# One mixer of a two-model block on one Trainium2 core: its gate chain, scores and sums placed among the projection panels

## The chip, the cores and the metric

One core of a Trainium2 chip runs the whole program. The metric is the device time of one execution in microseconds (us), the median of several. The engines are TensorE (PE, with its weight loads shown apart as PEld), VectorE (DVE), ScalarE (ACT), GpSimd (POOL) and SyncE (SP), which issues the weight transfers.

## The reference

The program is a chain: one attention and recurrence block with a mixture of experts, then four layers of feed-forward, mixer, feed-forward. The mixers of layers 0 and 3 are the ones changed here, so the changed code runs twice (`r` is 0 and 1). For one of them, with 256 tokens, 1024 channels, 4 heads, keys of 128 and values of 256 elements:

```python
def mlstm_mixer(x, w_in, b_if, conv_w, norm_g, w_out):
    proj = x @ w_in
    qk, v, o, if_pre = jnp.split(proj, [2 * H * dk, 2 * H * dk + H * dv, 2 * H * dk + 2 * H * dv], axis=-1)
    qk = jax.nn.silu(causal_depthwise_conv_2(qk, conv_w))
    if_pre = ML_GATE_CAP * jnp.tanh((if_pre + b_if) / ML_GATE_CAP)
    i_log, f_pre = jnp.split(if_pre, 2, axis=-1)
    f_log = jax.nn.log_sigmoid(f_pre)
    h = mlstm_chunkwise(q * dk ** -0.5, k, v, i_log, f_log)
    h = head_rms(h).reshape(B, T, H * dv) * norm_g
    return (h * jax.nn.sigmoid(o)) @ w_out

# inside mlstm_chunkwise, b = cumsum(f_log), m_t a running maximum, for one chunk:
    s = einsum('bhtd,bhsd->bhts', q, k) * exp(log_d - m_t)      # log_d[t, s] = b[t] - b[s] + i[s], masked
    den = sum(s)
    h = num / maximum(abs(den), exp(-m_t))                       # num = s @ v
```

The kernel takes all 256 tokens as one chunk, so it carries no state. `head_rms` divides each head's row by its root mean square.

## The kernel before

All data stays on chip between the parts. Every float32 weight arrives in panels of 1 MB (`raw`), is split by ACT into a rounded part (`w_hi`, L286) and by DVE into the rest (`w_lo`, L291), and is multiplied in three products (L321 to L323). A ring of RING = 3 slots holds the panels: the slot of panel p is loaded, split and used, and the split of panel p+3 (`act_ahead`, `dve_ahead`) waits until PE has done panel p. Each engine works through its own instructions in the order written, and waits on counted semaphores: `tensor_done` counts the results of PE, `lo_made` the panels split, `evacuated[i]` the reads of accumulator bank i. A result numbered n lies in `bank[n % 4]` and may be written when result n-4 has been read. Four more banks, `acc[0]` to `acc[3]`, hold the sums of the output projection and, at the joints between parts, the transposes of the norm.

A mixer has 16 panels: v0 to v3, q0 to q3 (these hold q and k, with 2 blocks of 128 columns each), o0 to o3, and four of the output weight. `pe_ml` (L1792) issues in this order: v0 and v1 in halves inside the norm (`pe_cross_halves`), v2, v3, q0 to q3, o0 to o3, and then a serial tail of small results named in `ML_ORDER`: `if` (gate logits of 8 columns, `pe_narrow`), `b` (cumulative sums, L1808 to L1810), `gT` (L1814), `Mt` (L1818), the exponents `D0` to `D3` of the decays (L1822, L1824), the scores `S0` to `S3` (L1829, L1830), the denominators `den` (L1835 to L1837), the numerators `num0` to `num3` (L1843 to L1845), four transposes `turn0` to `turn3` (L1851), and then the output panels out0 to out3 (`pe_out_panels`, rows of 512 into acc).

`act_ml` (L1859) reads each projection (L1866 for v, L1870 for q, the sigmoid L1872 for o) and splits the next panel right after; then it does the four silus (L1878), tanh, exp, ln (L1881 to L1885), the decays' exps (L1891 to L1893), |den| (L1897), the numerators scaled by 1/den (L1904, into `scratch`), the squares of those (L1910), and the rounded part of the gated output (`mix_hi`, L1917). `dve_ml` (L1924) makes w_lo after each split, the four-tap convolutions of q0 to q3 between (L1937, L1939), then `z`, `e1`, `nb`, `g`, `gT`, the running maximum and `nM` (L1951 to L1965), `Mt` (L1967), the four products score times decay (L1974), 1/den (L1979, L1980), the scaling by the norm (L1985, on `scratch`, all heads before `scaled` is signalled), gate times norm (L1991, `out0` to `out3`) and the rest of the gated output (`mix_lo`, L1999, `low0` to `low3`). `pool_ml` turns mean squares into reciprocal roots (L2011, L2013). The weights' transfers are issued by SP in panel order, each when the panel three before it has been split.

Of the kernel before, what the change touches and what calls it, by code (L numbers as in the profile page):

```python
# [26 lines left out]
EPS = 1e-6  # L27
# [126 lines left out]
def block_kernel(nc, d, out, consts, decays):  # L154

    ctx = ExitStack()
    with ctx:
# [1588 lines left out]
        def pe_out_panels(pe, c, panels, ready, src):  # L1746
# [7 lines left out]
            def last_ready(i):  # L1754
# [15 lines left out]
        ml_dve = Steps("ml_dve", ["cleared", "conv0", "conv1", "conv2", "conv3", "z", "e1", "g", "nM", "m", "rd",  # L1770
                                  "scaled"] + [f"out{j}" for j in range(4)] + [f"low{j}" for j in range(4)])
        ml_act = Steps("ml_act", ["silu0", "silu1", "silu2", "silu3", "tanh", "exp", "ln", "em", "ad", "squares"])
# [15 lines left out]

        def ml_moved(c):
            c.p += 4; c.e += 4 + len(ML_ORDER); c.n += len(ML_ORDER)  # L1790

        def pe_ml(pe, c, r):  # L1792
            pe_cross_halves(pe, c)
            pe_project(pe, c, 4, pe_columns_tok, first=2)
            c.p += 4; c.n += 4; c.e += 4
            pe_project(pe, c, 8, pe_columns_T)
            c.p += 8; c.n += 8; c.e += 8
            for key, j in ML_RES.items():
                n = c.n + j
                b = bank[n % BANKS]  # L1800
                if key == "if":
                    pe_narrow(pe, n, 44 + 8 * r, 8)
                    continue
                pe_result_free(pe, n)
                h = int(key[-1]) if key[-1].isdigit() else None
                if key == "b":
                    ml_act.wait(pe, "ln", r)
                    pe.matmul(b[:, 0:4], C("tri"), ml_nl[:, 0, :], start=True, stop=True)  # L1808
                    pe.matmul(b[:, 4:8], C("ones"), ml_nl[:, 0, :], start=True, stop=False)
                    last = pe.matmul(b[:, 4:8], C("tri"), ml_nl[:, 1, :], start=False, stop=True)  # L1810
                elif key == "gT":
                    ml_dve.wait(pe, "g", r)
                    for t in range(TT):
                        last = pe.matmul(b[0:4, t * P:t * P + P], ml_g[:, t, :], ident, start=True, stop=True)  # L1814
                elif key == "Mt":
                    ml_dve.wait(pe, "nM", r)
                    for t in range(TT):
                        last = pe.matmul(b[:, 4 * t:4 * t + 4], ml_nM[:, t * P:t * P + P], ident[:, 0:4],  # L1818
                                         start=True, stop=True)
                elif key[0] == "D":  # L1820
                    for at, cols in ((0, T), (T, P)):
                        pe.matmul(b[:, at:at + cols], ident[:, h:h + 1].to_broadcast([P, P]), ml_nM[:, T - cols:T],  # L1822
                                  start=True, stop=False)
                        last = pe.matmul(b[:, at:at + P], ident, C("neg_st"), start=False, stop=True)  # L1824
                elif key[0] == "S":
                    if h == 0:
                        ml_act.wait(pe, "silu3", r)
                    q, k = ml_qk[:, h, :], ml_qk[:, 4 + h, :]
                    pe.matmul(b[:, 0:T], k[:, 0:P], q, start=True, stop=True)  # L1829
                    last = pe.matmul(b[:, T:384], k[:, P:T], q[:, P:T], start=True, stop=True)  # L1830
                elif key == "den":
                    for h in range(4):
                        wait_evacuated(pe, c.n + ML_RES[f"S{h}"])
                        one = C("ones")[:, 0:1]
                        pe.matmul(b[:, h:h + 1], ml_S[:, h, 0:P], one, start=True, stop=True)  # L1835
                        pe.matmul(b[:, 4 + h:5 + h], ml_S[:, h, P:T], one, start=True, stop=False)
                        last = pe.matmul(b[:, 4 + h:5 + h], ml_S[:, h, T:384], one, start=False, stop=True)  # L1837
                elif key.startswith("num"):
                    if h == 0:
                        for back in range(9, 13):  # L1840
                            wait_evacuated(pe, c.n - back)
                    v = slice(h * ML_DV, h * ML_DV + ML_DV)
                    pe.matmul(b[:, 0:T], ml_S[:, h, 0:P], ml_v[:, 0, v], start=True, stop=True)  # L1843
                    pe.matmul(b[:, T:2 * T], ml_S[:, h, P:T], ml_v[:, 0, v], start=True, stop=False)
                    last = pe.matmul(b[:, T:2 * T], ml_S[:, h, T:384], ml_v[:, 1, v], start=False, stop=True)  # L1845
                else:
                    ml_dve.wait(pe, "scaled", r)
# [11 lines left out]
        def act_ml(act, c, r):  # L1859
            act_cross(act, c, norm_col(3 * r, 2))  # L1860
            for j in range(12):
# [5 lines left out]
                elif j < 8:  # L1867
                    if j == 4:
                        ml_dve.wait(act, "cleared", r)
# [1195 lines left out]
```

## Time and profile before

| | |
|---|---|
| median of 3 runs | 2969.29 us (2963.32, 2969.29, 2969.39) |
| the profiled execution, device time | 2963.17 us |
| its span | 2961.4 us |
| busy share of the span | PE 94%, PEld 88%, DVE 55%, ACT 45%, POOL 4% |
| chain of work that ended last | PE 87%, DVE 6%, ACT 4%, issue 1%, POOL 1% |
| mean granted TensorE clock | 0.967 of full |

The device time is the span and 1.8 us around it. The two mixers lie at about 788 to 941 us and 2608 to 2760 us of the span. A number in a row's "us" column is the time of a group that follows without a break; the same group in the second mixer has the same durations within 0.1 us. A granted clock of 1.00 is the upper of TensorE's two levels (2.4 GHz), 0.50 the lower (1.2 GHz); a number between is a mixture over the stretch.

### The profile page before, as it was taken

How to read it: one execution, taken by the hardware profiler on the slowest of the kernel's cores; microseconds unless marked ns; L12 is line 12 of the kernel's file. 1: busy time of each engine (PE TensorE's matmuls, PEld its weight loads, DVE VectorE, ACT ScalarE, POOL GpSimd, SP SyncE). 2: the span in 40 equal slices, each digit the busy share in tenths (PEclk: the TensorE clock that was granted, in tenths of full speed). 3: DMA queues.
4: the chain of work that ended last, by engine and by line, in shares of the span. 5: the costliest groups of instructions: out<-in, count | busy, mean ns of one | idle time of the engine just before them, and what ended most of it. 6: DMA issues, size and time to landing. Idle time of an engine off the chain costs nothing.

```text
span 2961.4 us, 51769 instructions
## 1 busy us (share of the span) xinstructions
PE 2770.3 (94%) x22402; PEld 2604.5 (88%) x22402; DVE 1634.4 (55%) x1725; ACT 1319.5 (45%) x1560; POOL 115.0 (4%) x185
## 2 busy tenths in 40 slices
PE   4789999899998999997998999999999999997999
PEld 4669999889997999997897999999979999997898
DVE  3445588854554445458765545446555454463544
ACT  3435477643444334447323434334334344344433
POOL 0000000000000000000211000000000000000000
PEclk9889999999988999998999999999999999998999
DMA  5207599845551555553301555555535555552453
GB/s 165 72 23 238 174 346 353 295 164 187 165 167 65 193 184 173 189 179 100 129 4 46 195 187 184 188 184 174 177 126 173 189 167 189 182 178 83 150 185 128
DMA packets 377590, 492.13 MB, mean 166 GB/s; under 512 B 18872, under 2 KB 337760, under 8 KB 377408
## 3 DMA queue, kind: packets, MB, share of 16 engines
q1 hardware_dynamic: 365280, 479.23, 48.6%
q0 software_dynamic: 2192, 7.73, 0.8%
q10 hardware_dynamic: 9936, 2.47, 0.4%
q8 instruction: 147, 2.41, 0.3%
q14 instruction: 35, 0.29, 0.0%
HBM read 488.35 MB, written 1.05 MB: 165 GB/s over the span
## 4 chain that ended last, share of the span: by engine, by line
PE 87%; DVE 6%; ACT 4%; issue 1%; POOL 1%; ACTq 1%; DMA 0%; DVEq 0%; POOLq 0%
PE bank L321 19%; PE bank L323 19%; PE bank L322 19%; PE acc L321 7%; PE acc L322 7%; PE acc L323 7%; PE bank L2462 1%; ACT w_hi L286 1%; PE acc L569 1%; DVE X L480 1%; DVE act_lo L501 1%; ACTq L827 1%; PE bank L2439 1%; PE bank L2450 1%; PE bank L569 1%
## 5 line engine op out<-in xcount | busy, mean ns | idle before, releaser
L291 DVE TENSOR_TENSOR w_lo<-raw,w_hi 128x2048 fp32r<-128x2048 f32 x360 | 824.2, 2292 | 790.3 <-ACT w_hi L286 790.1
L321 PE MATMUL bank<-act_hi,w_hi 128*128 128x256 f32 x3592 | 1019.4, 284 | 9.8 <-DVE act_lo L2714 7.7
L323 PE MATMUL bank<-act_hi,w_lo 128*128 128x256 f32 x3592 | 1018.6, 284 | 0.0
L322 PE MATMUL bank<-act_lo,w_hi 128*128 128x256 f32 x3592 | 1018.5, 284 | 0.0
L286 ACT ACTIVATE w_hi<-raw 128x2048 fp32r<-128x2048 f32 x360 | 688.1, 1912 | 511.4 <-PE acc L323 265.5
L321 PEld LDWEIGHTS bank<-act_hi,w_hi 128*128 128x128 f32 x3592 | 691.6, 193 | 13.3 <-issue 10.5
L322 PEld LDWEIGHTS bank<-act_lo,w_hi 128*128 128x128 f32 x3592 | 691.4, 192 | 2.9
L323 PEld LDWEIGHTS bank<-act_hi,w_lo 128*128 128x128 f32 x3592 | 691.4, 192 | 0.0
L321 PE MATMUL acc<-w_hi,mix_hi 128*128 128x512 f32 x928 | 366.0, 394 | 6.8 <-DVE mix_lo L1999 5.6
L322 PE MATMUL acc<-w_lo,mix_hi 128*128 128x512 f32 x928 | 364.8, 393 | 0.0
L323 PE MATMUL acc<-w_hi,mix_lo 128*128 128x512 f32 x928 | 363.8, 392 | 0.0
L321 PEld LDWEIGHTS acc<-w_hi,mix_hi 128*128 128x128 f32 x928 | 176.5, 190 | 42.5 <-issue 8.0
L323 PEld LDWEIGHTS acc<-w_hi,mix_lo 128*128 128x128 f32 x928 | 175.9, 190 | 37.8
L322 PEld LDWEIGHTS acc<-w_lo,mix_hi 128*128 128x128 f32 x928 | 176.5, 190 | 33.2
L704 ACT ACTIVATE silu_out<-bank 128x512 f32<-128x512 f32 x88 | 52.5, 597 | 299.7 <-PE bank L323 299.7
L321 PE MATMUL bank<-w_hi,act_hi 128*128 128x256 f32 x544 | 157.7, 290 | 1.2
L1506 DVE TENSOR_TENSOR w_lo<-raw,w_hi 128x2048 fp32r<-128x2048 f32 x57 | 130.6, 2292 | 49.8 <-ACT w_hi L1398 49.8
L322 PE MATMUL bank<-w_lo,act_hi 128*128 128x256 f32 x544 | 155.3, 285 | 0.0
L323 PE MATMUL bank<-w_hi,act_lo 128*128 128x256 f32 x544 | 155.0, 285 | 0.0
L1398 ACT ACTIVATE w_hi<-raw 128x2048 fp32r<-128x2048 f32 x57 | 109.0, 1913 | 38.7 <-PE bank L323 21.3
L749 DVE TENSOR_TENSOR gated<-silu_out,bank 128x512 f32<-128x512 f32 x88 | 60.5, 688 | 113.0 <-PE bank L323 113.0
L321 PE MATMUL bank<-w_hi,moe_xhi 128*128 128x256 f32 x384 | 109.6, 285 | 0.0
(492 smaller groups left out, 3252.3 us busy)
## 6 DMA issues: line engine op xcount, KB each, us to landing
raw<-in_ffn_w_gu SPq DMA_DIRECT2D x176, 1024.0 KB, 5.1
raw<-in_ffn_w_down SPq DMA_DIRECT2D x88, 1024.0 KB, 4.9
raw<-in_ml_w_in SPq DMA_DIRECT2D x24, 1024.0 KB, 5.4
raw<-in_rt_w_in SPq DMA_DIRECT2D x24, 1024.0 KB, 5.2
raw<-in_w_up SPq DMA_DIRECT2D x20, 1024.0 KB, 7.3
raw<-in_w_gate SPq DMA_DIRECT2D x19, 1024.0 KB, 6.8
raw<-in_w_down SPq DMA_DIRECT2D x18, 1024.0 KB, 6.6
moe_raw<-in_w_down SPq DMA_DIRECT2D x14, 1024.0 KB, 6.6
```

The source lines that it names most:

```text
L286: act.activation(w_hi[0:rows, slot, 0:size], raw[0:rows, slot, 0:size], ACT.Copy).then_inc(hi_made, 1)
L291: dve.tensor_tensor(w_lo[0:rows, slot, 0:size], raw[0:rows, slot, 0:size], w_hi[0:rows, slot, 0:size].bitcast(F32), ALU.subtract).then_inc ...
L321: pe.matmul(dst, l_hi, r_hi, start=start, stop=False)
L322: pe.matmul(dst, l_hi, r_lo, start=False, stop=False)
L323: return pe.matmul(dst, l_lo, r_hi, start=False, stop=stop)
L480: dve.scalar_tensor_tensor(x, scratch[:, t, cols], rstd[:, t:t + 1], x, ALU.mult, ALU.add).then_inc(x_quarter, 1)
L501: last = dve.scalar_tensor_tensor(act_lo[:, k, tok], turn_place(c, t, k), vecs[:, g + k:g + k + 1], act_hi[:, k, tok].bitcast(F32), ALU.mu ...
L569: last = pe.matmul(turn_place(c, t, k), X[:, t, k * P:k * P + P], diag[:, t, :], start=True, stop=True)
L704: act.activation(silu_out[:, h, :], bank[r % BANKS][:, :], ACT.Silu).then_inc(evacuated[r % BANKS], 1)
L749: dve.tensor_tensor(gated[:, h, :], silu_out[:, h, :], bank[b2][:, :], ALU.mult).then_inc(evacuated[b2], 1)
L1398: act.activation(w_hi[:, p % RING, :], moe_slab(p), ACT.Copy).then_inc(hi_made, 1)
L1506: dve.tensor_tensor(w_lo[:, p % RING, :], moe_slab(p), w_hi[:, p % RING, :].bitcast(F32), ALU.subtract).then_inc(lo_made, 1)
```

## The change

PE's order becomes: v0, v1, `if`, v2, v3, `b`, q0, `gT`, q1, `Mt`, D0, D1, q2, D2, D3, q3, o0, S0 to S3, o1, `den`, num0 to num3, o2, turn0 to turn3, o3, then the output panels as before. D, S and num of head h go to `acc[h]` and have no number in the ring of four banks; their readers signal by steps of `ml_act` and `ml_dve`. ACT and DVE are written out in the order that fits, each split of a panel standing where its projection's read stands (ACT) or where a line `ahead(...)` stands (DVE). The numerators stay in `acc[h]`: ACT takes the squares from there, scaled by 1/den (L1904 and L1910 become one pass), POOL multiplies the reciprocal root by 1/den, and one scaling by that product copies the numerators to `scratch`, heads 0 and 1 on ACT, heads 2 and 3 on DVE; each head's transposes wait for that head alone. `mix_hi` and `mix_lo` are made pair by pair. SP's order is unchanged.

```diff
@@ -1767,13 +1767,18 @@
...
+        ML_EV = [("v", 0), ("v", 1), ("if",), ("v", 2), ("v", 3), ("b",), ("q", 0), ("gT",), ("q", 1), ("Mt",), ("D", 0), ("D", 1),
+                 ("q", 2), ("D", 2), ("D", 3), ("q", 3), ("o", 0)] + [("S", h) for h in range(4)] + [("o", 1), ("den",)]
+        ML_EV += [("num", h) for h in range(4)] + [("o", 2)] + [("turn", j) for j in range(4)] + [("o", 3)]
...
+        ML_RES = {k: j for j, k in enumerate(k for k in ML_EV if k[0] not in ("D", "S", "num"))}
+        ML_PAN = {(x, j): 4 * i + j for i, x in enumerate("vqo") for j in range(4)}
+        ml_dve = Steps("ml_dve", ["cleared", "z", "e1", "g", "conv0", "nM", "conv1", "m", "conv2", "conv3"]
+                       + [f"S{h}" for h in range(4)] + ["rd", "scaled2", "scaled3"]
+                       + [x for j in range(4) for x in (f"out{j}", f"low{j}")])
+        ml_act = Steps("ml_act", ["tanh", "exp", "ln", "em"] + [f"D{h}" for h in range(4)] + [f"silu{j}" for j in range(4)]
+                       + ["ad"] + [f"squares{h}" for h in range(4)] + ["scaled0", "scaled1"] + [f"high{j}" for j in range(4)])
-        ML_ORDER = (["if", "b", "gT", "Mt"] + [f"D{h}" for h in range(4)] + [f"S{h}" for h in range(4)] + ["den"]
-                    + [f"num{h}" for h in range(4)] + [f"turn{j}" for j in range(4)])
-        ML_RES = {k: j for j, k in enumerate(ML_ORDER)}
...
         def ml_moved(c):
-            c.p += 4; c.e += 4 + len(ML_ORDER); c.n += len(ML_ORDER)
+            c.p += 12; c.n += len(ML_RES); c.e += len(ML_EV)
...
+            def project(x, j):
+                p = c.p + ML_PAN[x, j]
+                pe.wait_ge(lo_made, p + 1)
+                result(x, j)
+                done((pe_columns_tok if x == "v" else pe_columns_T)(pe, N[x, j] % BANKS, p % RING))
+
+            def decays(h):
+                b = acc[h]
...
+            pe_narrow(pe, N["if",], 44 + 8 * r, 8)
+            project("v", 2)
+            project("v", 3)
+            b = result("b")
+            ml_act.wait(pe, "ln", r)
...
+            done(pe.matmul(b[:, 4:8], C("tri"), ml_nl[:, 1, :], start=False, stop=True))
+            project("q", 0)
+            b = result("gT")
+            ml_dve.wait(pe, "g", r)
...
+            done(last)
+            project("q", 1)
+            b = result("Mt")
+            ml_dve.wait(pe, "nM", r)
...
+            done(last)
+            decays(0)
+            decays(1)
+            project("q", 2)
+            decays(2)
+            decays(3)
+            project("q", 3)
+            project("o", 0)
+            for h in range(4):
+                if h == 0:
+                    ml_act.wait(pe, "silu2", r)
+                elif h == 2:
+                    ml_act.wait(pe, "silu3", r)
+                ml_act.wait(pe, f"D{h}", r)
...
+            project("o", 1)
+            b = result("den")
+            ml_dve.wait(pe, "S3", r)
...
+            for h in range(4):
+                v = slice(h * ML_DV, h * ML_DV + ML_DV)
+                pe.matmul(acc[h][:, 0:T], ml_S[:, h, 0:P], ml_v[:, 0, v], start=True, stop=True)
+                pe.matmul(acc[h][:, T:2 * T], ml_S[:, h, P:T], ml_v[:, 0, v], start=True, stop=False)
+                done(pe.matmul(acc[h][:, T:2 * T], ml_S[:, h, T:384], ml_v[:, 1, v], start=False, stop=True))
+            project("o", 2)
+            for j in range(4):
...
+            project("o", 3)
...
+            def projected(x, j):
+                b = got(x, j)
...
+                read(last, x, j)
+                q = c.p + ML_PAN[x, j] + RING
+                act_split(act, q % RING, loads(q), E[x, j])
...
+            projected("v", 0)
+            projected("v", 1)
+            ml_dve.wait(act, "z", r)
...
+            projected("v", 2)
+            ml_dve.wait(act, "e1", r)
...
+            projected("v", 3)
+            projected("q", 0)
+            projected("q", 1)
+            ml_dve.wait(act, "m", r)
...
+            decays(0)
+            decays(1)
+            projected("q", 2)
+            decays(2)
+            decays(3)
+            projected("q", 3)
             for j in range(4):
                 ml_dve.wait(act, f"conv{j}", r)
...
+            projected("o", 0)
+            projected("o", 1)
+            b = got("den")
...
+                b = got("num", h)
+                    last = act.activation(ml_qk[:, 2 * h + t, :], b[:, t * T:t * T + T], ACT.Square,
+                                          scale=ml_rd[:, t, h:h + 1], accum_out=ml_ss[:, t, h:h + 1])
+                ml_act.done(last, f"squares{h}", r)
+            ml_pool.wait(act, "rs", r)
+            for h in range(2):
                 for t in range(TT):
-                    last = act.activation(ml_D[:, 0, 0:ML_DV], scratch[:, t, h * ML_DV:(h + 1) * ML_DV], ACT.Square,
-                                          accum_out=ml_ss[:, t, h:h + 1])
-                    if (h, t) != (3, 1):
-                        own_act(last)
-            ml_act.done(last, "squares", r)
-            for j in range(4):
+                    last = act.activation(scratch[:, t, h * ML_DV:(h + 1) * ML_DV], acc[h][:, t * T:t * T + T], ACT.Copy,
+                                          scale=ml_rs[:, t, h:h + 1])
+                ml_act.done(last, f"scaled{h}", r)
+            projected("o", 2)
...
+            high(0)
+            high(1)
+            high(2)
+            projected("o", 3)
+            high(3)
+            ml_moved(c)
             for j in range(2):
                 act_ahead(act, c.p + j, c.e + j)
...
+            ahead("v", 0)
+            b = got("if")
...
             ml_dve.done(dve.nop(), "z", r)
+            ahead("v", 1)
             ml_act.wait(dve, "exp", r)
...
+            ahead("v", 2)
+            ahead("v", 3)
+            b = got("b")
...
+            conv(0)
+            ahead("q", 0)
+            b = got("gT")
...
+            conv(1)
+            ahead("q", 1)
+            b = got("Mt")
...
             ml_dve.done(dve.nop(), "m", r)
+            conv(2)
+            ahead("q", 2)
+            conv(3)
+            ahead("q", 3)
...
+                b = got("S", h)
+                ml_act.wait(dve, f"D{h}", r)
...
+            ahead("o", 0)
+            ahead("o", 1)
             ml_act.wait(dve, "ad", r)
...
+            dve.nop().then_inc(evacuated[N["den",] % BANKS], 1)
             ml_pool.wait(dve, "rs", r)
+            for h in range(2, 4):
                 for t in range(TT):
+                    last = dve.tensor_scalar(scratch[:, t, h * ML_DV:(h + 1) * ML_DV], acc[h][:, t * T:t * T + T],
+                                             ml_rs[:, t, h:h + 1], None, ALU.mult)
+                ml_dve.done(last, f"scaled{h}", r)
+            ahead("o", 2)
...
+                wait_evacuated(dve, N["o", j])
+                b = got("turn", j)
...
+            for j in range(3):
+                out(j)
+                low(j)
+            out(3)
+            low(3)
+            ahead("o", 3)
...
-            ml_act.wait(pool, "squares", r)
-            own_pool(pool.tensor_scalar(ml_rs[:, :, :], ml_ss[:, :, :], 1.0 / ML_DV, EPS, ALU.mult, ALU.add))
-            flat = ml_rs[:, :, :].rearrange("p t h -> p (t h)")
-            ml_pool.done(pool.tensor_tensor(flat, flat, exponent[:, 0:8], ALU.pow), "rs", r)
-            c.p += 12; c.n += 12; c.e += 12
+            ml_act.wait(pool, "squares3", r)
+            ml_dve.wait(pool, "rd", r)
+            flat = lambda a: a[:, :, :].rearrange("p t h -> p (t h)")
+            own_pool(pool.tensor_scalar(flat(ml_ss), flat(ml_ss), 1.0 / ML_DV, EPS, ALU.mult, ALU.add))
+            own_pool(pool.tensor_tensor(flat(ml_ss), flat(ml_ss), exponent[:, 0:8], ALU.pow))
+            ml_pool.done(pool.tensor_tensor(flat(ml_rs), flat(ml_ss), flat(ml_rd), ALU.mult), "rs", r)
             ml_moved(c)
-            c.hi += 4
+            c.p += 4; c.e += 4
```

## Rows read from the trace of the kernel before

**Rows 1.** Windows from:to: length, PE, PEld, DVE, ACT, POOL busy, granted clock, DMA.

```profile
809.60:867.20 57.60, 57.60 (x483) 57.60 (x481) 37.64 (x43) 25.26 (x21) 0.00 (x0) 1.00 0.58 184
867.20:916.50 49.30, 31.20 (x176) 28.43 (x174) 13.59 (x33) 23.39 (x51) 1.86 (x2) 0.70 0.13 43
...
2686.80:2736.10 49.30, 31.20 (x176) 28.46 (x174) 13.59 (x33) 23.39 (x51) 1.86 (x2) 0.72 0.13 43
```

**Rows 2.** Timeline of PE: start, us, instruction, idle before and its releaser.

```profile
882.89 0.99 PE L1818 MATMUL bank<-con,ml_nM 128*128 128x4 f32 x4 [1.63 <-DVE ml_nM L1965]
...
888.89 0.60 PE L1822 MATMUL bank<-ml_nM,con 128*128 128x256 f32 x2
...
889.99 0.60 PE L1829 MATMUL bank<-ml_qk 128*128 128x256 f32 x2
...
892.61 0.28 PE L1835 MATMUL bank<-con,ml_S 128*128 128x1 f32 x2
...
895.21 0.68 PE L1843 MATMUL bank<-ml_v,ml_S 128*128 128x256 f32 x2
...
910.11 3.65 PE L1851 MATMUL bank<-con,scratch 128*128 128x128 f32 x16 [9.47 <-DVE scratch L1985]
916.55 0.77 PE L321 MATMUL acc<-w_hi,mix_hi 128*128 128x512 f32 x1 [2.79 <-DVE mix_lo L1999]
```

**Rows 3.** Windows of PE alone: length, PE busy, granted clock, DMA share, GB/s.

```profile
870.30:874.50 4.20, 4.20 (x21) 0.50 0.32 97
...
916.50:921.50 5.00, 4.95 (x12) 0.50 0.00 0
...
797.50:801.50 4.00, 3.97 (x23) 0.64 0.52 163
1143.60:1147.00 3.40, 3.40 (x28) 1.00 0.53 173
1470.30:1474.50 4.20, 4.19 (x74) 0.50 0.95 316
```

**Rows 4.** PE's waits over the span: us in total, times, longest.

```profile
PE acc L569 <- ACT gated L427: 48.5, 17, 11.3
...
PE bank L2439 <- DVE rw_xx L2820: 4.9, 1, 4.9
```

**Rows 5.** Timeline of ACT, first mixer.

```profile
867.40 0.60 ACT L1872 ACTIVATE ml_o<-bank 128x512 f32<-128x512 f32 x1 [3.36 <-PE bank L323]
867.89 1.90 ACT L286 ACTIVATE w_hi<-raw 128x2048 fp32r<-128x2048 f32 x1
869.81 1.28 ACT L1878 ACT_TABLE_LOAD   x1
871.11 2.19 ACT L1878 ACTIVATE ml_qk<-ml_qk 128x512 f32<-128x512 f32 x4
...
901.40 0.41 ACT L1910 ACTIVATE ml_D<-scratch 128x256 f32<-128x256 f32 x1
...
905.50 0.19 ACT L1910 ACTIVATION_READ_ACCUMULATOR ml_D<-scratch 128x1 f32 x1
```

**Rows 6.** Timeline of DVE, first mixer.

```profile
831.72 0.61 DVE L1937 TENSOR_SCALAR ml_qk<-ml_in,vecs 128x256 f32<-128x256 f32 x2
832.36 2.72 DVE L1939 SCALAR_TENSOR_TENSOR ml_qk<-ml_in,vecs,ml_qk 128x256 f32<-128x256 f32 x6
...
869.83 2.29 DVE L291 TENSOR_TENSOR w_lo<-raw,w_hi 128x2048 fp32r<-128x2048 f32 x1 [3.47 <-ACT w_hi L286]
...
881.31 0.41 DVE L1962 COPY ml_gT<-bank 4x256 f32<-4x256 f32 x1 [1.19 <-PE bank L1814]
...
907.77 2.19 DVE L1985 TENSOR_SCALAR scratch<-scratch,ml_rs 128x256 f32<-128x256 f32 x8 [11.62 <-POOL ml_rs L2013]
911.23 0.88 DVE L1991 SCALAR_TENSOR_TENSOR ml_o<-bank,vecs,ml_o 128x256 f32<-128x256 f32 x2 [1.27 <-PE bank L1851]
```

**Rows 7.** DVE scaling from a bank elsewhere: ns min/median/max, first and last start.

```profile
L2219 DVE TENSOR_SCALAR scratch<-bank,rt_rs x8: 743/746/752, 2161.6 to 2177.7; 128x512 f32<-128x512 f32 x8
```

More of the change, by code:

```diff
@@ L1796, in pe_ml @@
[L1796 to L1812, printed above, removed]
-                    for t in range(TT):
[L1814 to L1847, printed above, removed]
-                    for m in range(2):
-                        for t in range(TT):
-                            k = 2 * h + m
-                            last = pe.transpose(b[:, m * T + t * P:m * T + t * P + P],
-                                                scratch[:, t, k * P:k * P + P], ident)
-                last.then_inc(tensor_done, 1)
@@ new lines, in pe_ml @@
+            project("o", 2)
+            for j in range(4):
+                b = result("turn", j)
+                if j < 2:
+                    ml_act.wait(pe, f"scaled{j}", r)
+                else:
+                    ml_dve.wait(pe, f"scaled{j}", r)
+                for m in range(2):
+                    for t in range(TT):
+                        k = 2 * j + m
+                        last = pe.transpose(b[:, m * T + t * P:m * T + t * P + P], scratch[:, t, k * P:k * P + P], ident)
+                done(last)
@@ L1943, in dve_ml, with got, read @@
[L1943 to L1949 removed]
+            def got(*key):
+                dve.wait_ge(tensor_done, E[key])
+                return bank[N[key] % BANKS] if key in N else acc[key[1]]
+            def read(last, *key):
+                last.then_inc(evacuated[N[key] % BANKS], 1)
@@ new lines, in ahead, with conv @@
+            def ahead(x, j):
+                q = c.p + ML_PAN[x, j] + RING
+                dve_split(dve, q, q % RING)
+            def conv(j):
+                wait_evacuated(dve, N["q", j])
+                for tap in range(4):
+                    for k in (2 * j, 2 * j + 1):
+                        src, w = ml_in[:, k, tap:tap + T], V("ml_conv", (4 * r + tap) * 8 + k)
+                        if tap == 0:
+                            last = dve.tensor_scalar(ml_qk[:, k, :], src, w, None, ALU.mult)
+                        else:
+                            last = dve.scalar_tensor_tensor(ml_qk[:, k, :], src, w, ml_qk[:, k, :], ALU.mult, ALU.add)
+                    if tap < 3:
+                        own(last)
+                ml_dve.done(last, f"conv{j}", r)
@@ L1986, in dve_ml, with out @@
-            ml_dve.done(last, "scaled", r)
-            for j in range(4):
-                b, read = result(f"turn{j}")
+                    last = dve.tensor_scalar(scratch[:, t, h * ML_DV:(h + 1) * ML_DV], acc[h][:, t * T:t * T + T],
+                                             ml_rs[:, t, h:h + 1], None, ALU.mult)
+                ml_dve.done(last, f"scaled{h}", r)
+            ahead("o", 2)
+            def out(j):
+                wait_evacuated(dve, N["o", j])
+                b = got("turn", j)
```

166 lines of the change are left out of this document (72 added, 94 removed).

## The prediction, made before the changed kernel was run

> **What bounds the kernel now.** I read three views. The stretches first: from 809.6 us, where PE has finished v0 and v1, to 867.2 it works without a gap at the upper clock through ten panels (57.6 us, so 5.76 each), and ACT and DVE are busy 25.3 and 37.6 us of it. From 867.2 to the first output panel at 916.5 it is busy 31.2 of 49.3 us, at a mean clock of 0.70; the second mixer repeats this (31.2 of 49.3) [rows 1]. So a mixer has 18.1 us of idle PE, and the rest of its tail partly at the lower clock. The PE timeline says what the tail waits for: 9.47 us before the transposes, for the scaling by the norm; 2.79 before the output panels, for `mix_lo`; 1.63 before `Mt`; the rest of the 18.1 before `b` and `gT` [rows 2]. Each wait is a chain of short ACT, DVE and POOL work in which PE has nothing else to do. The clock comes third: the narrow product begins at 867.2 behind panels at the upper level, and from 870.3 to its end at 874.5 it runs at the lower, and the output panels run their first 5.0 us at the lower level [rows 3]. What matters is whether this work, put among the ten panels, finds cover, and what the panels then wait for.
>
> **What the full-clock work of the tail is.** At the upper clock one head of D takes 1.10 us (888.89 to 889.99), the four S 2.6, `den` 2.6, the four num 5.4 (895.21 to 910.11 less the wait of 9.47) [rows 2]. Groups like `Mt` take 0.99 at the lower clock [rows 2]; at the upper they are not shown, so each of `b`, `gT` and `Mt` lies between half and the whole, 0.5 to 1.0, and I take 0.5, for `b` 0.7. The transposes, 3.65 at the lower clock, come to between 1.8 and 3.65; I take 2.0 since the panels before them are at the upper level.
>
> **Walk, part 1: from 809.6 to the end of q0.** Before, v2 starts at 809.6; now `if` does. It took 7.3 us behind full-clock panels (867.2 to 874.5), ending at the lower level, and so will it here. v2 then starts low. Panels of this kind ran 5.0 us low after 916.5 before the clock rose, which costs half of that time [rows 3]; I charge 1.8, between 1 and 3. Sum: 7.3 + 1.8 + three panels (17.3) + `b` 0.7 = 27.1. Cover: tanh and exp run inside v2; ln stands behind v2's read and split on ACT (0.2 after PE, 0.49 to the split, 1.9, a table load of 1.28 [rows 5]), some 4.1 after v2's end, 1.6 before `b` asks for it. Behind ln's wait on ACT stands only v3's read. `g` stands on DVE behind the w_lo of v3's turn, 5.4 after v3's end against 6.5 at which `gT` asks: 1.1 to spare.
>
> **Part 2: from q0's end (call it 0) to o1's end.** A refill now: ACT reads at 0.2, splits at 0.7 to 2.6, DVE follows at 2.63 for 2.3 us [rows 5, 6], so a panel's successor is ready 4.9 after its end, and is wanted at 11.5 (two panels later) or more: 6.6 us to spare. PE does `gT` and q1 until 6.3. But DVE does conv0 first (it waits for the read of q0, 0.8; 3.4 long), then w_lo (2.2), and only then copies `gT` at 6.5. From that copy to `Mt` it is 1.58 (881.31 to 882.89) [rows 2, 6]. So `Mt` starts at 8.0: **a stall of 1.8 us**, once a mixer. Gaps of about 2 us stand before the norm's transposes in nearly all of the 17 joints [rows 4]; after some the clock fell (797.5: 0.64 over 4 us), after most it did not (1143.6: 1.00) [rows 3]. I charge 0.7. Then `Mt` 0.5, D0 and D1 2.2, q2, D2 and D3 2.2, q3, o0: 30.2. DVE, behind conv1 (3.4) and q1's w_lo, reads `Mt` at 13.6; ACT's em (with a table load) and the first exps end at 17.1, so q2 is read 0.45 late. conv3 ends at 28.7. Silus 0 to 2 follow q3's split and a table load and end near 30.0, the fourth at 30.6 [rows 5]: S0 is asked for at 30.2, so it just comes. S 2.6 and o1 5.76 end part 2 at 38.6; with the clock charge 39.3. The ring: the latest w_lo is q1's, ready 7.2 after q1's end instead of 4.9; the panel it serves is wanted 18 after. SP's transfers follow w_lo in the same order and are never later than the panels need.
>
> **Part 3: from o1's end (U) to o3's end.** PE: `den` 2.6, num 5.3 (the first one paid 0.1 for its start), o2: U+13.6. ACT reads o1, splits (to U+2.6), takes |den| at U+2.8; DVE's w_lo ends at U+4.9, 1/den is ready at U+5.3. Squares: eight took 4.29 us (901.40 to 905.69) [rows 5], here U+5.4 to 9.8, the last numerators being there at U+8. POOL took 2.1 from the squares to the next engine's start (905.69 to 907.77 [rows 5, 6]) and gets one small operation more, 0.2 to 0.5: rs at U+12.3. ACT scales heads 0 and 1 until U+13.9, DVE heads 2 and 3 until U+14.0. The 9.47 us wait is thus covered by o2, with nothing to spare. turn2 and turn3 end at U+15.5, turn3 having waited for ACT's read of o2 (behind its scalings). Then comes the **second stall**: o3 is numbered four behind turn0 and needs `out0` done, and DVE has the w_lo of o2's turn in front of it. ACT splits after its read of o2, U+14.4 to 16.3; w_lo to U+18.6; `out0` 0.9 and its signal [rows 6]; o3 starts at U+19.65, 4.2 us idle. After a wait of 4.95 the clock stood at 0.50 for 4.2 us [rows 3, 4], worth 2.1; I charge 2.0. o3 ends at U+25.4, or U+27.4 with it. In these 5.8 us `out0` to `out2` and their low parts are done, so out0's panel starts at once at the upper clock; `out3` and `low3` end 4 us later, out2's weights 6 us later, both wanted 10 later.
>
> **Sum.** New: 27.1 + 39.3 + 27.4 = 93.8 us from 809.6 to the first output panel. Before: 916.55 - 809.60 = 106.95. That is 13.15 less, and the output panels no longer start low, 2.5 in the first mixer; I take 2.1 as the mean of both, since the moment of recovery varies. 15.3 a mixer, 30.5 in all: **2963.2 - 30.5 = 2932.7** on the profiled execution's own time. Two of the three unprofiled runs lie 6 us above it (2969.3), one at it. The median after may fall in either place, 2932.7 or 2938.8; I name **2935**. Changes within 0.2% (6 us) are what a measurement of this kernel can't tell from none.
>
> **Rivals.**
> - *Stalls and clock cost half.* The clock recovers early behind `if`, o3 waits 2 us (DVE's w_lo in the shadow), no dip at `Mt`: 5 more a mixer, 2922 to 2928. For it: the charges of 1.8, 0.7 and 2.0 are estimates. Against: the order of DVE fixes the wait of o3. 12%. The end of this road is 81.5 us for the stage (panels 57.6, the rest 23.9 at full clock and no idle), 2908.
> - *The tight handovers slip.* ln to `b`, `g` to `gT`, silu2 to S0 and squares to turn0 have 1.6, 1.1, 0.2 and 0 us. If each is late by 1 to 2 and the clock falls once more, 7 to 8 a mixer go: 2948 on own time, to 2954. For it: two have no slack, and semaphore steps of 0.05 to 0.1 are not in my walk. Against: a slip at S0 or turn0 moves both queues alike. 20%. Here belongs the source of the scaling: from SBUF it took 2.19 for eight passes, 0.27 each, from a bank 0.747 for twice the columns [rows 6, 7], so some 0.4 a pass, which I used. The Trainium skill, VectorE: DVE Perf Modes, section "Why PSUM operands drop a tier", speaks against the move: a float32 tensor_scalar has its double rate from SBUF only. By it the four passes on DVE cost 0.5 more than from SBUF, and head 3 would be the last before turn3; the trace agrees on the rate.
> - *The panels wait for their splits; nothing is gained.* Each of seven w_lo stands behind an awaited result; were the waits 6.6 us longer than in my walk, each panel would stall. That takes 15 us a mixer and gives 2963 to 2969. My largest delay is 2.3. 5%.
> - *Slower: the clock stays low among the panels.* The short products and the stalls, spread over the stage, keep PE at the lower level. Panels at the lower level take twice as long, so it decides where 27% of the 57.6 us of panel work runs low (15.3); at half it is 28.8 - 15.3 = 13.5 slower a mixer, 2990. Against: PE ran D, S, `den` and num back to back at the upper clock, and after a 4.95 us wait it was low for 4.2 us only [rows 3, 4]. 3%.
>
> **How the numbers follow.** The forecast has 60%. Its own bounds, clock charges 1 to 3, 0 to 1.7 and 1 to 2.5, give 2927 to 2938 on own time, to 2944 with the 6 us. 10% of the slip and half of the first rival must be in too: 2921 to 2951. Faster 0.92, same 0.05, slower 0.03.
>
> **What would show it.** Right: PE's waits in the stage sum to about 6 to 7 us, before `Mt` (1.8, behind `nM`) and before o3 (4.2, behind `out0`'s bank); none before the transposes above 0.5; the narrow product again falls to the lower clock after 3 us; the first output panel starts some 93 us after v1's end. Wrong: waits before S0 or turn0 above 1 us; lo_made as PE's releaser among the panels; a mean clock under 0.85 over the stage.

## The result, and the profile after

The changed kernel takes 2935.01 us (median of 4 runs, 2929.75 to 2936.62); the kernel before, in the runs beside it, 2968.51. The ratio is 0.9888, 95% interval 0.987 to 0.9905: faster by 1.1%. The profiled execution took 2936.62 us. Two lines of the page, busy time and the chain that ended last:

```profile
PE 2768.2 (94%) x22402; PEld 2605.3 (89%) x22402; DVE 1632.4 (56%) x1717; ACT 1314.4 (45%) x1552; POOL 115.2 (4%) x187
...
PE 87%; DVE 6%; ACT 4%; issue 1%; POOL 1%; ACTq 1%; DMA 0%; POOLq 0%; DVEq 0%
```

PE issues the same 22402 products as before, and ACT and DVE have 8 instructions fewer each; what went is PE's idle time and its time at the lower clock. Where: PE's transposes of the norm (L569) stand at every joint between two parts, so the distance from one joint to the next times a part. The first mixer of the changed kernel lies between these two starts (timeline of PE; start, duration):

```profile
797.21 1.16 PE L569 MATMUL acc<-gated,X 128*128 128x128 f32 x8 [1.97 <-ACT gated L427]
...
925.55 1.16 PE L569 MATMUL acc<-gated,X 128*128 128x128 f32 x8
```

That is 128.34 us, against 143.49 before (797.53 to 941.02): 15.15 less. The second mixer went from 141.44 to 126.89: 14.55 less. Together 29.7, where the two spans differ by 26.6; the other stretches, unchanged in their code, gave back 3.1, in four steps of 1.3 to 2.2 against two of 1.4 the other way (below).

Inside the first mixer, stretches of the changed kernel (length; PE, PEld, DVE, ACT, POOL busy; granted clock; DMA share; GB/s), which answer to [rows 1]: the gate logits with v2; then all to the end of o1; then `den` to the end of o3:

```profile
809.30:825.10 15.80, 15.80 (x99) 15.80 (x98) 4.58 (x4) 4.10 (x5) 0.00 (x0) 0.68 0.46 136
825.10:875.70 50.60, 49.33 (x400) 48.34 (x399) 32.45 (x49) 27.01 (x32) 0.00 (x0) 1.00 0.42 128
875.70:903.50 27.80, 23.80 (x163) 22.97 (x162) 10.96 (x17) 12.24 (x28) 2.07 (x3) 0.88 0.31 110
```

From the end of v1 to the first output panel it is 94.2 us, where it was 106.95. And PE's waits of that stage, first mixer (us in total, times, longest), where [rows 2] had 18.1 us of idle time:

```profile
PE bank L321 <- DVEq L2069: 4.0, 1, 4.0
PE bank L1842 <- DVE ml_nM L2030: 1.3, 1, 1.3
```

Two waits are left, the two of the walk. The timeline of PE places them (start, duration, idle before):

```profile
816.94 0.56 PE L321 MATMUL bank<-w_hi,act_hi 128*128 128x256 f32 x1
...
845.17 0.58 PE L1842 MATMUL bank<-con,ml_nM 128*128 128x4 f32 x4 [1.27 <-DVE ml_nM L2030]
...
889.35 1.91 PE L1884 MATMUL bank<-con,scratch 128*128 128x128 f32 x16
895.26 0.55 PE L321 MATMUL bank<-act_hi,w_hi 128*128 128x256 f32 x1 [4.00 <-DVEq L2069]
903.50 0.40 PE L321 MATMUL acc<-w_hi,mix_hi 128*128 128x512 f32 x1
```

The transposes follow o2 with no wait at all, where 9.47 us stood. o3 starts at 895.26 after 4.00 idle. What DVE does meanwhile (its timeline):

```profile
887.18 1.66 DVE L2056 TENSOR_SCALAR scratch<-acc,ml_rs 128x256 f32<-128x256 f32 x4 [6.21 <-POOL ml_rs L2097]
891.98 2.29 DVE L291 TENSOR_TENSOR w_lo<-raw,w_hi 128x2048 fp32r<-128x2048 f32 x1 [3.14 <-ACT w_hi L286]
894.19 0.87 DVE L2066 SCALAR_TENSOR_TENSOR ml_o<-bank,vecs,ml_o 128x256 f32<-128x256 f32 x2
```

The bank that o3 needs is freed by the last of these lines; its input, turn0, had been there since about 889.9, and DVE stood 3.14 us in wait for a split that `out0` doesn't need.

The clock, in windows of PE alone (length, busy, granted clock, DMA share, GB/s): low from 2.7 us into the narrow product to 5.3 us into v2, low again over the end of the wait and most of o3, and at its upper level where the output panels begin, which ran low before [rows 3]:

```profile
812.00:822.20 10.20, 10.20 (x49) 0.50 0.46 127
...
893.90:900.70 6.80, 5.44 (x25) 0.50 0.48 157
...
903.50:908.50 5.00, 5.00 (x24) 1.00 0.00 2
```

### The profile page after: what moved, and what is told of

It is laid out like the page before. It is cut to its first block, busy times and chain, and to the rows that moved or that the text cites. A ratio compares the mean times of both kernels' runs of the same rounds, so it can differ in the third digit from the quotient of the medians.

```text
span 2934.8 us, 51755 instructions
## 1 busy us (share of the span) xinstructions
PE 2768.2 (94%) x22402; PEld 2605.3 (89%) x22402; DVE 1632.4 (56%) x1717; ACT 1314.4 (45%) x1552; POOL 115.2 (4%) x187
## 4 chain that ended last, share of the span: by engine, by line
PE 87%; DVE 6%; ACT 4%; issue 1%; POOL 1%; ACTq 1%; DMA 0%; POOLq 0%; DVEq 0%
PE bank L321 20%; PE bank L323 19%; PE bank L322 19%; PE acc L321 7%; PE acc L322 7%; PE acc L323 7%; PE bank L2545 1%; ACT w_hi L286 1%; PE acc L569 1%; DVE X L480 1%; DVE act_lo L501 1%; ACTq L827 1%; DVE w_lo L291 1%; PE bank L2522 1%; PE bank L2533 1%
## 5 line engine op out<-in xcount | busy, mean ns | idle before, releaser
L321 PEld LDWEIGHTS bank<-w_hi,act_hi 128*128 128x128 f32 x544 | 108.7, 200 | 3.7 <-issue 3.0
```

What stands on the lines that cost most here:

```text
L321: pe.matmul(dst, l_hi, r_hi, start=start, stop=False)
```

## The experiments

Times from joint to joint, first and second mixer, in us. In the first, several kernels also have a fall of the clock right at the leading joint, worth 1.4; the second has none there, so it is the cleaner column. The time of one whole execution is no measure of an edit: it moves by several us with falls of the clock elsewhere.

| kernel | first | second | second against changed |
|---|---|---|---|
| before | 143.49 | 141.44 | +14.55 |
| changed | 128.34 | 126.89 | 0 |
| changed, again | 128.20 | 127.74 | +0.85 |
| `out0` ahead of w_lo | 121.83 | 120.50 | -6.39 |
| scan ahead of convolution | 128.45 | 127.86 | +0.97 |
| gate logits woven into v2 | 122.18 | 121.12 | -5.77 |
| all three | 115.88 | 115.89 | -11.00 |
| gate chain only | 130.19 | 131.84 | +4.95 |
| norm only | 136.13 | 134.74 | +7.85 |
| two scalings | 126.15 | 124.83 | -2.06 |
| all three, again | 117.28 | 115.91 | -10.98 |
| two edits | 115.76 | 115.72 | -11.17 |
| two edits, `den` woven | 117.04 | 115.69 | -11.20 |
| all three, `den` woven | 114.22 | 114.18 | -12.71 |

**`out0` ahead of the w_lo.** Is the wait at o3 DVE's order, or the end of a chain?

```diff
-            ahead("o", 2)
...
             for j in range(3):
                 out(j)
+                if j == 0:
+                    ahead("o", 2)
                 low(j)
```

> DVE makes out0 (0.9 us) before the w_lo that stands in front of it. Theory A (DVE's own order holds the bank that o3 needs, and the idle time costs clock besides): PE's wait before o3 falls from 4.00 us to 0 to 0.5, o3 runs at the upper clock and takes 5.8 instead of 8.2 us, the output panels start 6.0 to 6.4 us earlier in each mixer, 12 to 13 us in all. Theory B (the wait is set by the chain of squares, root and scaling, and would only move): the wait stays above 2 us, before the transposes or before o3, and less than 5 us are gained in all.

One execution: 2916.27 us. Windows of PE over o2 and the transposes, then o3, then the first output panel:

```profile
883.40:891.20 7.80, 7.80 (x67) 1.00 0.20 82
891.20:897.00 5.80, 5.80 (x50) 1.00 0.27 89
897.00:902.00 5.00, 5.00 (x24) 1.00 0.32 112
```

No idle time and no low clock: o3 takes 5.8 us instead of 8.2, and the mixers are 6.5 and 6.4 shorter, 12.9 in all, which is theory A (the first lies 0.1 above its 6.4). Of the 6.4, 4.0 are the wait and 2.4 what it did to the clock. The whole execution is 20.4 shorter than that of the changed kernel; the other 7.4 lie in four stretches that the edit doesn't touch, each with less time at the lower clock, and are not its gain.

**The scan ahead of the convolution.** The order of `nM` and `conv0` changes places in the list of steps, and

```diff
-            conv(0)
-            ahead("q", 0)
             b = got("gT")
...
+            conv(0)
+            ahead("q", 0)
             conv(1)
```

> DVE copies gT and makes nM before the convolution of q0 and the w_lo that stood ahead of them. Theory A (queue order): the wait of 1.27 us before Mt is gone and nothing later moves, 1.3 us less in each mixer from the end of v1 to the first output panel, 2.5 in all. Theory B (the work put off comes due later): Mt starts earlier, but PE waits as long for w_lo, the silus or S3 further on, 0 gained.

One execution: 2935.82 us. The wait before `Mt` is gone: the page has one wait left in the stage, the 4.0 at o3. But the mixers got 0.1 and 1.0 longer. Windows of PE: o1, `den`, the first numerators, the rest of them:

```profile
868.40:874.30 5.90, 5.90 (x53) 1.00 0.51 188
874.30:876.90 2.60, 2.60 (x27) 1.00 0.87 356
876.90:880.30 3.40, 3.40 (x9) 0.50 0.11 7
880.30:884.00 3.70, 3.70 (x19) 1.00 0.72 277
```

Up to the end of the scores everything runs 1.47 us earlier (868.43 against 869.90). Then, behind the 2.6 us of one-column `den` products, the clock is at the lower level for 3.4 us, which costs 1.7. In the second mixer it falls 2.1 us after `den` has begun, for 6.8 us, which costs 3.3; there the fall at o3 is half as long and gives 0.9 back. Neither theory stands as written: no later wait took the gain, the clock did, in both mixers. In the changed kernel's two profiled executions the same products passed without a fall in three mixers and had one in the fourth (1.7 lost there and 0.9 given back at o3, the +0.85 of the table). I come back to it with the last two kernels.

**The gate logits woven into v2.** In `pe_ml`, per token tile and k, three narrow products and then v2's three:

```diff
-            pe_narrow(pe, N["if",], 44 + 8 * r, 8)
-            project("v", 2)
...
+            for t in range(TT):
+                for k in range(KT):
...
+                    last = split_product(pe, bi[:, t * 8:t * 8 + 8], act_hi[:, k, tok], act_lo[:, k, tok],
+                                         narrow_hi[:, k, a:a + 8], narrow_lo[:, k, a:a + 8], k == 0, k == KT - 1)
...
+                    last = split_product(pe, bv[:, t * PW:t * PW + PW], act_hi[:, k, tok], act_lo[:, k, tok],
+                                         w_hi[:, slot, w], w_lo[:, slot, w], k == 0, k == KT - 1)
```

> The 48 narrow products of the gate logits are issued in threes between the threes of v2 instead of in one block ahead of it. Theory A (the block of narrow products lets the clock fall, and v2 pays for it): both together take 11.2 us at the upper clock instead of 7.6 + 8.2, the chain to ln then ends 0.4 to 0.9 us after v3, so 3.7 to 4.3 us less in each mixer, 7.4 to 8.6 in all. Theory B (narrow products keep the clock low wherever they stand, or the block costs no clock): the granted clock over v2 stays below 0.9 and at most 2 us are gained in all.

One execution: 2922.93 us. Both together, and v3 behind them, in windows of PE:

```profile
808.10:819.20 11.10, 11.10 (x98) 1.00 0.41 128
819.20:825.00 5.80, 5.80 (x51) 1.00 0.39 117
```

11.1 us at the upper clock instead of 15.8 at 0.68: theory A. `b` follows v3 at once, so ln, which I had 0.4 to 0.9 late, was in time. The mixers gained 6.2 and 5.8, more than the 3.7 to 4.3 expected: 4.7 is this edit, the rest is clock elsewhere that this execution happened not to lose (at the joint ahead of the first mixer, and in half of the fall at o3 in the second).

**All three.**

> All three edits together. Theory A (they act in different places): the gains add up, 10.5 to 12 us in each mixer, so 21 to 24 us less than the changed kernel and 52 to 57 less than the kernel before, near 2912. Theory B (one critical chain behind all): the largest alone, 12 to 13 us.

2910.22 us, ratio to before 0.9827 (0.9805 to 0.985), which is 51.2 less than the kernel before on that chip, a little under the 52 expected. The mixers lose 12.5 and 11.0 us; 1.4 of the 12.5 is the fall at the leading joint, which this execution had not. So the first two edits add up (6.4 and 4.7), and they act in different places. What the scan adds to them the comparison with two edits says, below: nothing so far.

**Gate chain only.** Which part of the change brought what? PE's order `if` v2 v3 `b` q0 `gT` q1 `Mt` q2 q3 o0 to o3, then D, S, `den`, num, turn; the norm as in the changed kernel. The core of it:

```diff
+            project("q", 2)
+            project("q", 3)
+            project("o", 0)
+            project("o", 1)
+            project("o", 2)
+            project("o", 3)
             decays(0)
             decays(1)
-            project("q", 2)
             decays(2)
             decays(3)
-            project("q", 3)
-            project("o", 0)
```

> Only the gate chain stands among the panels; D, S, den, num and the transposes follow o3 as before the change, with the one scaling of the changed kernel. Theory A (walk of the queues: D 4.4, S 2.6 with a short wait for D's exps, den and num 7.8, some 4.4 of wait for squares, root and scaling, transposes, low0 ready 23 to 25 us after o3; the gate chain costs 12.9 among the panels): a mixer from joint to joint is 3 us longer than in the changed kernel and 12 shorter than before. So the placing of D, S and num behind the stall at o3 brings only 3 of the 15 us. Theory B (the tail's waits were what counted and they come back): 7 us or more longer than in the changed kernel.

One execution: 2950.31 us. 1.9 and 5.0 us longer than the changed kernel. The two differ by luck with the clock: the first mixer was spared the fall at the joint (1.4) and 3.4 us of low clock in the gate stage (1.7), and without that it is 5.0 as well. That is 2 more than theory A's 3, and short of theory B's 7. The wait before the transposes is 4.4 as walked. What the walk has not is a wait of 0.7 before `den`, and the clock, which in the second mixer is low for 6.8 us from 1.7 us into `den` and for 3.4 at the transposes. So placing D, S and num among the panels is worth 5 of the 14.6 us, not 3.

**Norm only.** PE's order of before, the new norm.

```diff
-            pe_narrow(pe, N["if",], 44 + 8 * r, 8)
             project("v", 2)
             project("v", 3)
...
+            project("o", 3)
+            pe_narrow(pe, N["if",], 44 + 8 * r, 8)
```

> PE's order is that of the kernel before; only the norm is changed (squares out of the accumulators, one scaling on two engines, transposes head by head, mix_hi and mix_lo pair by pair). Theory A: the wait before the transposes falls from 9.5 to 4.4 us, that before the output panels from 2.8 to under 0.5, 7 to 8 us less in each mixer than before, about half of the whole gain. Theory B (the norm's chain only gives the time to another wait): less than 3 us in each mixer.

One execution: 2947.27 us; 7.4 and 6.7 less than before in the mixers. Waits of PE in the first mixer:

```profile
PE bank L1883 <- ACT scratch L1959: 4.4, 1, 4.4
PE bank L1835 <- ACT ml_nl L1940: 3.7, 1, 3.7
...
PE acc L321 <- DVE mix_lo L2074: 0.2, 1, 0.2
```

4.4 instead of 9.5 and 0.2 instead of 2.8, as walked; a new wait of 0.7 stands before `den`. So the norm's part alone, without any new placing, is nearly half of the gain. Its own pieces (squares out of the accumulators, one scaling on two engines, transposes head by head, output pair by pair) were not run one by one in this order. In the second mixer, whose column has no spared falls, the shares are 6.7 for the norm, 2.9 more for the gate chain among the panels, 5.0 more for D, S and num (differences of the table's rows; the first mixer has 7.4, 5.9 and 1.9).

**Two scalings.** The changed kernel with 1/den applied on ACT, squares from SBUF, and DVE scaling all heads.

```diff
-                    last = act.activation(ml_qk[:, 2 * h + t, :], b[:, t * T:t * T + T], ACT.Square,
-                                          scale=ml_rd[:, t, h:h + 1], accum_out=ml_ss[:, t, h:h + 1])
+                    last = act.activation(scratch[:, t, h * ML_DV:(h + 1) * ML_DV], b[:, t * T:t * T + T], ACT.Copy,
+                                          scale=ml_rd[:, t, h:h + 1])
...
-            for h in range(2, 4):
+            for h in range(4):
```

> The changed kernel with two scalings again: numerators by 1/den into SBUF on ACT, squares from there, DVE scales all four heads. Theory A (in the new order DVE's w_lo sets the start of o3, so the longer chain is mostly covered): PE waits some 2.2 us before the transposes and 2.5 before o3 instead of 0 and 4.0, a mixer is 0.7 to 2 us longer. Theory B (the one scaling carries the gain here too): 5 us or more longer in each mixer.

One execution: 2935.34 us. Both theories miss: the mixers are 2.2 and 2.1 us shorter than with one scaling. Waits of PE, and the clock from o2's end over o3:

```profile
PE bank L321 <- DVEq L2065: 2.4, 1, 2.4
PE bank L1881 <- DVE scratch L2053: 1.4, 1, 1.4
```

```profile
883.00:900.00 17.00, 13.21 (x106) 1.00 0.29 102
890.00:902.00 12.00, 9.04 (x69) 1.00 0.27 89
```

The idle time is nearly the same, 3.8 against 4.0, but in two pieces, and the clock never falls; o3 takes 5.8 us. In the changed order the work saved on ACT and DVE was worth nothing, since DVE's w_lo stands at the end either way (it starts at 891.88 here and at 891.98 in the changed kernel), and joining two waits to one cost some 2.4. With the w_lo in front of `out0` the one scaling loses 2.1 us a mixer; with `out0` first the two scalings were not run.

**The changed kernel, two edits, and `den` woven.** Three kernels, timed in turn on one chip; the two edits are `out0` first and the woven gate logits.

> The changed kernel as it is, to be timed beside the next two: 0.9888 of the kernel before, between 0.987 and 0.9905.

2934.95 us, 0.9891 (0.9873 to 0.9908).

> out0 ahead of the w_lo, and the gate logits woven into v2; the convolution and the maximum in the order of the changed kernel. Theory A (the two act apart, as the single looks say: 6.4 and 6.0 us a mixer): 12 to 12.5 us less in each mixer, 24 to 25 less than the changed kernel, ratio to before 0.981 to 0.983. Theory B (moving the scan first helps too, and was hidden by the clock): 2 us or more slower than with all three edits.

2909.81 us, 0.9813 (0.9795 to 0.9831): faster than before by 1.9% and than the changed kernel by 25.1 us, as theory A has it (12.6 and 11.2 in the mixers, where it has 12 to 12.5; 1.4 of the 12.6 is again the joint). From just ahead of the gate logits to the end of the first output panel, in one window of PE:

```profile
806.00:897.00 91.00, 89.73 (x701) 1.00 0.44 139
```

One wait of 1.27 us and no fall of the clock. Against all three edits (2910.22, ratio 0.9827) there is no loss, so theory B's 2 us are not there. Its reason, a gain of the scan hidden by the clock, is another matter: the last kernel below shows it.

> As the one before, and the 24 products of one column of den stand in threes among the second half of o1, with |den| and 1/den ahead of the splits that follow o1. Theory A (the den block of 2.6 us lets the clock fall in some executions, 1.7 us each time, as behind den in the second look; woven it cannot): no fall of the clock between o1 and o2, equal work otherwise, 0 to 3.4 us less than without this edit, 1 to 2 in the median. Theory B (the clock falls by chance of phase whatever stands there): no difference, and the falls are found as often.

The edit puts three `den` products behind each second group of three of o1's second half:

```diff
+                    if m == 1 and k % 2:
+                        h = k // 2
...
+                        pe.matmul(bd[:, h:h + 1], ml_S[:, h, 0:P], one, start=True, stop=True)
```

2910.22 us, 0.98 (0.9781 to 0.9818): no difference from the two edits alone, and the 1 to 2 us that theory A expected are not seen. The profiled executions can't decide: neither of the two had a fall between o1 and o2. In the two kernels with the scan first, the clock fell during `den` or right behind it in all four mixers; in six profiled executions of kernels without it and with `den` in one block behind o1, in one of twelve. In the two kernels that keep `den` in the tail behind a wait of 0.7 us (gate chain only, norm only), it fell in all four, 1.7 to 4.0 us after `den` had begun.

**`den` woven where the clock fell.** All three edits again, and the same with `den` woven, timed in turn on one chip.

> All three edits a second time. In the two kernels that have the scan first, the clock fell behind den in all four mixers seen; in the others in one of twelve. Theory A (it belongs to this order of work): it falls again in both mixers, 115.9 us from joint to joint. Theory B (chance of the moment): it falls in none or one, and a mixer without the fall takes 114.3 to 114.6 us.

2913.16 us, 0.9814 (0.9795 to 0.9833). In its profiled execution the clock fell in both mixers again, and 115.91 us is the second mixer, as theory A has it (117.28 the first, with a fall at its leading joint). Windows of PE, first mixer: the end of `den` and the first numerator (`den` ends at 874.9), the next ones, the last ones with the start of o2:

```profile
873.50:875.90 2.40, 2.40 (x20) 1.00 0.50 205
875.90:879.30 3.40, 3.40 (x10) 0.50 0.25 46
879.30:883.00 3.70, 3.70 (x23) 1.00 0.59 241
```

> All three edits, and den woven into the second half of o1. Theory A (the block of one-column products lets the clock fall in this order, and woven it cannot): no fall from v2 to the first output panel, PE has no wait there, a mixer takes 114.3 to 114.6 us from joint to joint, 1.2 to 1.5 less than with any kernel so far; 2.5 to 3 us less than all three edits. Theory B (the fall needs no den block): the clock falls between o1 and o2 here too and nothing is gained.

2907.7 us, 0.981 (0.9788 to 0.9831). One window of PE from just ahead of the gate logits to the end of the first output panel:

```profile
806.00:897.00 91.00, 91.00 (x706) 1.00 0.44 139
```

PE is busy in every one of the 91 us and never leaves the upper clock; the mixers take 114.22 and 114.18, so theory A stands: the scan's 1.3 us is real, and the block of `den` products took it back through the clock. Why it does so in this order, six times in six, and once in twelve in the other, the runs don't say. The medians are 5.5 us apart (2913.16 and 2907.7), but the single times overlap (2906.38 to 2914.64 and 2905.13 to 2917.58), and they can't be told from those of two edits either (0.981 against 0.9813); only the profiled mixers show the 1.5 us.

## Why the prediction was right, step by step

The range held the time, and the walk held the mechanism. By its own steps, first mixer:

- *Part 1, 27.1 forecast, 28.1 measured* (809.30 to 837.37). The narrow product took 7.64 for 7.3, v2 8.15, so the clock's charge was 2.4 where I had 1.8: the stretch of low clock lasted into v2 for 5.3 us. In it v2's products of 256 columns came every 0.213 us, behind it every 0.120, so the low level took 1.8 times as long for them, not the twice that I used throughout. `b` took 0.6 for 0.7. The term was within its bounds of 1 to 3. The covers held: ln ended at 829.2, `b` was asked for at 830.85, so 1.6 to spare as said.
- *Part 2, 39.3 forecast, 38.4 measured.* The wait before `Mt` was 1.27 for 1.8, and my charge of 0.7 for the clock behind it was not incurred in either mixer. S0 came when asked for: it needs the first three silus, the four took from 865.51 to 867.70, so the third ended at about 867.15, and S0 began at 867.36 with no wait.
- *Part 3, 27.4 forecast, 27.8 measured.* No wait before the transposes; 4.00 for 4.2 before o3, behind `out0`'s bank; 2.4 for 2.0 lost to the clock in o3.
- *The output panels start at the upper clock.* Forecast 2.1 a mixer; L569 comes 22.05 us after their start where it was 24.47: 2.4. In the second mixer it is 22.06 for 23.76, 1.7, since these panels do differ between the mixers before; the mean is the 2.1.
- Sum of the two mixers: 30.5 forecast, 29.7 measured. The parts were off by up to 1 us, mostly in the clock charges (0.6 too low in part 1, 0.7 too high in part 2, 0.4 too low at o3), and these cancelled: the three charges were 4.8 us for 4.5. That they did is luck.
- *The signs.* The waits sum to 5.3 us, a little under the 6 to 7 named; both stand where they were said, and there is none before the transposes. The narrow product fell to the lower clock after 2.7 us, and the first output panel came 94.2 us after v1's end for "some 93".
- *A reading that was wrong.* I put gaps of about 2 us at nearly all of the 17 waits of the norm's transposes. Ten of them are of that length (1.95 to 1.98); the clock fell at four of the ten before and at five of the ten after. Nothing in the sum changes by it.
- *The rest of the kernel.* I had it unchanged. It gave back 3.1 us in the profiled execution: the clock fell at three joints at which it hadn't before (1.4 each) and stayed up at two at which it had fallen; the largest step, 2.2, lies inside another part (1318.8 to 1602.7). The window behind one joint, before and after:

```profile
1819.90:1823.40 3.50, 3.42 (x28) 1.00 0.64 167
```

```profile
1805.30:1808.70 3.40, 3.40 (x17) 0.50 0.66 198
```

  The feed-forward part behind the norm is then 188.1 us long instead of 186.7. In other runs such falls stand at other joints, so I take this for scatter of an execution, not for a cost of the change. It is of the size of the spread between runs (6.9 us among the four).
- That the median is 2935.01 and I wrote 2935 is partly luck: I split 6 us between two clusters of the times before, and the measured medians fell by 33.5 us while the two profiled executions differ by 26.6. With 29.7 for the mixers, both are inside that scatter.
- *Rivals.* Handovers slipping: none did, by any measurable amount. Weights as releaser among the panels: no such wait in the stage. A low clock among the panels: the gate stage and o3 only, mean 0.91 from 806 to 903.5 (the falls were mine, and in the sum). The rival of smaller stalls did not happen by itself, but the experiments made it: one stall and the narrow block went for 25.1 us in the medians (two edits), and with the other stall and the `den` block gone too, the stage from v1's end to the first output panel took 81.42 us (808.10 to 889.52). The rival's end of the road was 81.5 us and 2908; the median was 2907.7, on another chip than the changed kernel's.
- The source of the scaling. On "VectorE: DVE Perf Modes" in the Trainium skill, section "Why PSUM operands drop a tier": the trace agrees. Four passes from the accumulators took 1.66 us (L2056), 0.41 apiece, against 0.27 from SBUF [rows 6], 0.56 more for the four where I had 0.5; and it cost nothing, since they end at 888.84 and the transposes could not begin before 889.35.

What I had wrong in kind showed in the experiments, not in the forecast: I priced the clock by the length of a wait. The two scalings show that nearly the same idle time costs 3.8 us in two pieces and 6.4 in one.

## What to carry to other kernels

When serial small work is put among wide products, walk every in-order queue that it passes: here the remaining waits both came from DVE work placed ahead of the one short step that PE needed, and moving one line ahead of another was worth 6.4 us a mixer. Look at what a block of very narrow products does to TensorE's clock and to the wide products behind it; woven in threes among wide ones the gate logits cost their own time only (11.1 us with v2, all at the upper clock). And before crediting a shortened chain, ask which queue ends last after it: a saving in front of it may join two waits into one that costs more.

## What the runs showed of the hardware

- With 48 products of 8 columns back to back and PE busy without a gap, the granted clock went from the upper to the lower level 2.7 us after their start; in all 16 mixers profiled with this block it fell, 2.2 to 4.6 us after the start. v2's wide products behind it ran low for another 5.3 us. Woven among wide products the same 48 left it at 1.00 over 11.1 us.
- A block of one-column products of 2.6 us had the clock fall in it or up to 1.4 us behind it in six mixers of six in one order of work, and in one of twelve in the other. In the tail it fell in four mixers of four where a wait of 0.7 us stood before the block, and in none of two without that wait (the kernel before). With the products woven into a wide panel it fell in none of four.
- A wait of 4.00 us before o3 cost the clock in all eight mixers that had it (3.4 to 6.8 us at the lower level); waits of 1.3, 1.4 and 2.4 us in this stage never did, while waits of 2.0 us ahead of the norm's transposes did at four joints of ten in the kernel before and at five of ten in the changed one.
- The 16 transposes took 1.91 us at the upper clock, 3.65 at the lower. In the second mixer before, they were all that PE did between 2720.3 and 2736.1, and the clock rose from the lower to the upper level at 2734.0, 0.6 us after their end.
